# Transposing both heads' probabilities ahead of the previous step's weighting in a dilated attention on one Trainium2 core

## The reference

```python
s = jnp.einsum('bdnqhc,bdnkhc->bdnhqk', qb, kb, preferred_element_type=jnp.float32)
s = s * (HEAD_DIM ** -0.5) + bias.astype(jnp.float32)
s = jnp.where(valid[None, None, :, None], s, NEG)
mx = jnp.max(s, axis=-1, keepdims=True)
e = jnp.exp(s - mx)
den = jnp.sum(e, axis=-1)
num = jnp.einsum('bdnhqk,bdnkhc->bdnqhc', e, vb.astype(jnp.float32))
```

## Time and profile before

| what | value |
|---|---|
| median of 3 runs | 1308.84 us (1307.89 to 1314.82) |
| the profiled execution's own time | 1307.89 us |
| its span, first to last instruction | 1306.2 us |
| PE busy | 1161.2 us, 89% of the span |
| DVE, ACT, POOL busy | 400.4, 328.7, 150.2 us |
| mean granted TensorE clock | 0.947 |

### The profile page before, as it was taken

How to read it: one execution, slowest core, us unless ns; L and a number is a source line. 1 busy time by engine, 2 the same in 40 slices (tenths; PEclk the granted TensorE clock), 3 DMA queues, 4 the chain that set the end, 5 groups by cost and what they waited for, 6 DMA issues and landing times.

```text
span 1306.2 us, 14695 instructions
## 1 busy us (share of the span) xinstructions
PE 1161.2 (89%) x5678; PEld 615.5 (47%) x5678; DVE 400.4 (31%) x934; ACT 328.7 (25%) x643; POOL 150.2 (11%) x147
## 2 busy tenths in 40 slices
PE   6999999999989999765899993989869697899997
PEld 3444445666656666633355552443323233344443
DVE  0322212201225666421175554341101010022443
ACT  2132322000006767322021110111111011135343
POOL 0100000000012122200001113621111010000000
PEclk9999999999998999788899995999989798999999
DMA  8211400103022100679931115599898989931331
GB/s 279 67 48 48 124 25 21 49 1 113 1 94 77 40 27 16 210 220 292 345 108 65 65 61 207 189 335 390 316 390 331 389 313 359 344 145 48 103 115 37
DMA packets 62771, 209.26 MB, mean 160 GB/s; under 512 B 14302, under 2 KB 28030, under 8 KB 46832
## 3 DMA queue, kind: packets, MB, share of 16 engines
q1 hardware_dynamic: 51648, 181.96, 39.9%
q0 software_dynamic: 10528, 26.37, 5.5%
q10 hardware_dynamic: 528, 0.00, 0.0%
HBM read 189.71 MB, written 25.42 MB: 165 GB/s over the span
## 4 chain that ended last, share of the span: by engine, by line
PE 75%; DMA 15%; DVE 4%; issue 2%; SPq 2%; ACT 1%; POOL 0%; ACTq 0%; POOLq 0%; DVEq 0%
PE pair L1721 13%; PE pair L1777 12%; PE pair L2057 9%; PE pair L2164 8%; DMA R<-in_w_up 8%; PE pair L1969 7%; PE pair L2079 4%; DMA R<-in_cache_v 4%; PE pair L1804 3%; PE pair L1817 3%; PE pair L1830 3%; PE pair L2145 2%; DMA R<-in_x_sample 1%; PE pair L2044 1%; PE pair L1998 1%
## 5 line engine op out<-in xcount | busy, mean ns | idle before, releaser
L2057 PE MATMUL pair<-R 128*32 128x512 f32 (+2 forms) x896 | 173.5, 630 | 38.4 <-DMA R<-in_w_up 36.2
L1721 PE MATMUL pair<-R 128*128 128x512 f32 x384 | 170.6, 601 | 0.8 <-DVE R L1190 0.8
L1777 PE MATMUL pair<-R 128*128 128x352 f32 x576 | 170.8, 459 | 0.4 <-ACT kts L911 0.4
L1777 PEld LDWEIGHTS pair<-R 128*128 128x128 f32 x576 | 109.3, 190 | 61.0 <-ACT kts L911 0.5
L2057 PEld LDWEIGHTS pair<-R 128*32 128x32 f32 (+2 forms) x896 | 60.4, 134 | 135.1 <-issue 131.5
L1969 PE MATMUL pair<-R 128*128 128x512 f32 x256 | 115.3, 605 | 0.3 <-DVE R L1400 0.3
L1721 PEld LDWEIGHTS pair<-R 128*128 128x128 f32 x384 | 72.8, 193 | 87.2 <-issue 85.9
L2164 PE MATMUL pair<-R 128*128 128x512 f32 x256 | 111.5, 593 | 1.7 <-ACT R L1103 1.7
L1557 DVE TENSOR_TENSOR R<-pair,R 128x256 f32<-128x256 f32 x23 | 9.8, 424 | 265.1 <-ACT R L1051 265.0
L2079 PE MATMUL pair<-R,bias_s 128*32 128x512 f32 (+2 forms) x448 | 83.5, 595 | 0.5 <-ACT bias_s L1055 0.5
L2164 PEld LDWEIGHTS pair<-R 128*128 128x128 f32 x256 | 47.9, 190 | 59.2 <-issue 59.1
(11 more groups left out here) (286 smaller groups left out, 1245.5 us busy)
## 6 DMA issues: line engine op xcount, KB each, us to landing
R<-in_w_gate SPq DMA_DIRECT2D x32, 1024.0 KB, 9.6
R<-in_w_up SPq DMA_DIRECT2D x32, 1024.0 KB, 12.1
R<-in_w_down SPq DMA_DIRECT2D x32, 1024.0 KB, 8.2
R<-in_x_prompt SPq DMA_DIRECT2D x16, 512.0 KB, 3.5
R<-in_cache_k SPq DMA_DIRECT2D x8, 1024.0 KB, 8.0
R<-in_cache_v SPq DMA_DIRECT2D x8, 1024.0 KB, 18.2
R<-y_dram SPq DMA_DIRECT2D x16, 512.0 KB, 4.6
R<-in_w_in SPq DMA_DIRECT2D x3, 2048.0 KB, 17.0
```

Of the source, the lines that this page charges most:

```text
L1721: last = mm(bk[4 + part][0:n, :], xTs[a.u][:, c, 0:n], wA[:, c, AD * part:AD * part + AD], start=(c == 0), stop=(c == DC - 1))
L1777: last = mm(bk[b][:, 0:n], wB[q % 2][:, c, which, :], xT[:, c, lo:lo + n], start=(c == 0), stop=(c == DC - 1))
L2057: last = mm(bk[2 + u][r, :].rearrange("p (w f) -> p w f", w=2), xgT[u][:, c, r], wgu[s][:, :, c, :], start=(c == 0), stop=(c == DC - 1))
```

## The change

PE's order in iteration n becomes score(n), trans_p(n-1, 0), trans_p(n-1, 1), weigh(n-2). `trans_p(n)` now does both heads in one function. Nothing else changes: the numbering of the bank uses, the waits of each use, the work of ACT, DVE, POOL and SP, and the number of instructions stay.

```diff
-        def trans_p(n, hh):
+        def trans_p(n):
             i = STEPS[n][1]
-            use = tp_uses(n) + hh * (-(-(i + 1) // 4))
-            pe.wait_ge(S("exp_done"), 2 * n + hh + 1)
-            for j0 in range(0, i + 1, 4):
-                m = min(4, i + 1 - j0)
-                if use >= 2:
-                    pe.wait_ge(S("tp_free"), use - 1)
-                for j in range(m):
-                    last = pe.transpose(bk[4 + use % 2][:, P * j:P * j + P], E[n % 2][hh][:, P * (j0 + j):P * (j0 + j) + P], ident[:, :])
-                last.then_inc(S("tp_full"), 1)
-                use += 1
+            use = tp_uses(n)
+            for hh in range(2):
+                pe.wait_ge(S("exp_done"), 2 * n + hh + 1)
+                for j0 in range(0, i + 1, 4):
+                    m = min(4, i + 1 - j0)
+                    if use >= 2:
+                        pe.wait_ge(S("tp_free"), use - 1)
+                    for j in range(m):
+                        last = pe.transpose(bk[4 + use % 2][:, P * j:P * j + P], E[n % 2][hh][:, P * (j0 + j):P * (j0 + j) + P], ident[:, :])
+                    last.then_inc(S("tp_full"), 1)
+                    use += 1
...
         for n in range(NSTEP):
             score(n)
             if n >= 1:
-                trans_p(n - 1, 0)
+                trans_p(n - 1)
             if n >= 2:
                 weigh(n - 2)
-            if n >= 1:
-                trans_p(n - 1, 1)
-        trans_p(NSTEP - 1, 0)
+        trans_p(NSTEP - 1)
         weigh(NSTEP - 2)
-        trans_p(NSTEP - 1, 1)
         weigh(NSTEP - 1)
```

## The result

The changed kernel took 1323.42 us (median of 7 runs, 1317.77 to 1327.12), the old one beside it 1309.70 us (7 runs). The ratio is 1.0092 with an interval of 1.0062 to 1.0120: slower, by 12 us, where 6.7 was forecast, and outside the range given. The profiled execution, an eighth, took 1333.01 us, more than any of the seven, so its total is read with care; its stages are read one by one.

The account below looks back on a forecast made before the run. The prediction took PE's pace to bound the attention, with PE busy 126.2 of 133.9 us. Its terms, 9.2 - 1.8 - 0.7 = +6.7 us, put on the median 1308.84, gave 1315.5 us, range 1311.5 to 1320.

Parts of the forecast that it names:

- Point 1: Attention steps with five to eight blocks: head 1's transposes wait for ACT's copy of the first bank, +9.2 us.
- Point 2: Attention steps with one to four blocks: one change of PE tiling mode less, 0.15 us in 12 steps, -1.8 us.
- Point 3: End of the attention: earlier transposes let ACT's last copy and exponential run earlier, -0.7 us.
- only one wait returns: Old attention: PE's only recurring wait is 1.23 us for DVE, at the start of pairs 1, 2 and 3.
- The sum for the attention: Whole attention: bank waits less saved mode changes and the earlier end, +6.7 us.
- I carry the sum through one to one: Stages after the attention: the total grows by the same 6.7 us, with 2 us each way for clock steps.
- Fewer changes of mode: Rival, attention: first bank copied in time, so the order only saves, 4.8 us in all, to 1304; chance 0.04.
- ACT comes late: Rival, short attention steps: head 1's exponential is not ready for its transposes, 3.6 us more, to 1319; chance 0.20.
- Absorbed downstream: Rival, sample stage: transfers starting at fixed times hide the later attention, result within 2 us of 1308.8; chance 0.08.

Follow-up runs that it names:

- r11: The changed kernel with five and six blocks shared more evenly between the two banks, on PE and ACT; ratio 1.0047 to the old kernel.
- r3: The old kernel with the new order only for steps with five to eight blocks; ratio 1.0063 to the old kernel.
- r1: The changed kernel again, no edit, for a second profile; ratio 1.0052 to the old kernel.
- r10: The old kernel again, no edit, for its profile; its one run took 1320.48 us, its attention 134.7 us.
- r4: The old kernel and order, with each weighting of the eight-block steps done twice, same output; ratio 1.0039 to the old kernel.
- r8: The old kernel and order, with each weighting of the eight-block steps done twice, a second sample; ratio 1.0077 to the old kernel.
- r2: The old kernel with the new order only for steps with one to four blocks; ratio 0.9984 to the old kernel.
- r6: The changed kernel again, no edit, a third sample; ratio 1.0094 to the old kernel.
- r7: The changed kernel again, no edit, a fourth sample; ratio 1.0068 to the old kernel.

## Why the prediction was right in its mechanism and missed the time

**Point 1, the bank's turn.** Right, with its size. The four long steps of a pair grew by 0.44, 0.56, 0.66 and 0.77 us (4.34 to 4.78, 5.43 to 5.99, 4.79 to 5.45, 4.13 to 4.90) where 0.44, 0.55, 0.66 and 0.76 stood in the sum. r11 shows that the copy sets it, r3 that it stands alone.

**Point 2, the saved change of mode.** Right in size: 0.15 us in the steps of four, three and two blocks (3.48 to 3.33, 2.83 to 2.68, 2.18 to 2.03), nothing at a pair's start, where score(8k+1) still waits for DVE.

**Point 3, the end.** Near: 5.76 to 5.01 us. But the transposes of the last two-block step lie inside this stretch, so their 0.15 was counted twice, in point 2 and here: the forecast for the stretch was 0.85 in all, and 0.75 was measured. A wait that I had overlooked made up for it; "only one wait returns" was not true. In the third pair of the old kernel the weighting of three blocks waits for ACT's copy:

```profile
485.49 0.49 PE pair L1817 x3
...
486.34 0.50 ACT R L960
486.88 0.88 PE pair L1830 x12
```

That iteration took 2.38 us instead of 2.18, and 2.03 in the new order: 0.20 more saved. The parts are then 11 x 0.15 + 0.20 + 0.75 = 2.6 us, for 2.5 forecast, so the closeness of this sum is in part luck.

**The sum for the attention.** +6.7 forecast, +6.6 and +6.7 measured, like against like. In the first profile of the changed kernel 0.9 more came from the clock in iteration 1.

**What failed is the step "I carry the sum through one to one", with its 2 us each way.** The first measurement had 12 us and the four together about 10 by their ratios, so 3 to 5 us came on top of the attention's (in r1 alone nothing did: 7 us in all). Part of what can come on top is seen: 0.9 us where step 0's transposes fall before the clock's rise, with the old kernel as well (r10). The sample stage took 113.8, 114.8 and 115.3 us in three profiles of the old kernel and 117.9, 115.6, 113.7 and 117.1 in four of the changed one; the means are 1.4 us apart and the two sets overlap, so this is not settled. It was 115.1 and 114.8 in r4 and r8, which end the attention as late, and 117.2 and 117.3 in r3 and r11, which have the new order in the long steps; so if the difference is real, it is not lateness alone. The largest piece that can come on top is the stall: with it the experts' stage took 381.0 us on average (nine profiles), without it 367.2 (four), and it comes to the old order too. How many of the timed executions had it is not known, as they were not profiled, so what share of the 3 to 5 us it has is not shown. I had read one profile, which had none, and so took the stages behind the attention as fixed lengths; their scatter is larger than the change. A further 0.9 us of the miss is the old kernel itself, whose median beside the changed one was 1309.70, where the forecast started from 1308.84. The range should have been about twice as wide upwards.

**The rivals.** Fewer changes of mode do save time, 0.15 us each in r2's steps, but 1.8 us in all against 9.2. The Trainium skill, "TensorEngine Tiling (Array Packing)", section Key Properties, says that a change of tiling mode drains TensorE; the trace agrees so far as each change of mode costs 0.15 us; the draining itself is not seen in it. "ACT comes late" did not occur in the changed kernel and occurred in r2 for a reason that I had not seen: mixing the two orders. "Absorbed downstream" did not occur: each of the four measurements of the changed kernel is slower than the old one beyond its interval.

**Open.** Whether a later end of the attention makes the stall more frequent on a chip where the old kernel mostly runs without it. On such chips the old kernel had none in two profiles; the changed kernel had it in its first and lacked it in r6, and r11 lacked it. The times hint that it does: where every profile has the stall, the changed kernel was slower by 7 and 9 us (r1, r7), about the attention's 6.6, and elsewhere by 12 us both times (the first result and r6). The intervals overlap, so this is not shown, and no run with the late end in the old order was made on such a chip. And what the stall is: the records show PE's work done and ACT released 7 us later, and nothing that I read in that stretch explains it.

## What to carry to other kernels

Before two runs of work that share a small ring of PSUM banks are put side by side, ask what covered the copy between them; the price is first transpose to copy, plus the copy, plus the hand-over, less what is still issued meanwhile, and it is greatest where little is left to issue. A place where the kernel already does what the change would do everywhere, such as the first step of a pipeline, gives that price from the old profile. Take a second profile of the unchanged kernel before trusting the stages behind the change: here its experts' stage alone took 366, 369 and 378 us in three.

## What the runs showed of the hardware that was not expected

The stall: in nine of thirteen profiles, of both orders, ACT started on block 1 of the experts' stage 6.9 to 7.4 us after the recorded (modelled) end of the matmul whose semaphore it waits for, and 11.4 us after it in the two profiles with the repeated weighting, where it is 0.04 us without the stall. The experts' stage took 378 to 384 us instead of 364 to 371. All eight profiles of the two chips where r1 to r4 and r7 to r10 ran have it, whatever the kernel; of the other five one has. And in the five profiles where step 0's transposes started 2 to 3 us before the granted clock rose, iteration 1 (with iteration 0) took 12.9 to 13.0 us, in the others 11.9 to 12.1; in the thirteen traces the rise lies anywhere from 398 to 402 us.
